# The second half of a modulation summed over k on GpSimd instead of TensorE, in a two-layer mixer kernel

## The reference

```
c_act, cc_act = silu(c), silu(c_ctx)            # two vectors of 2048
mod   = c_act @ w_mod + b_mod                   # w_mod: 2048 x 12288, float32, 100 MB
mod_c = cc_act @ w_mod + b_mod
sh1, sc1, gt1, sh2, sc2, gt2 = split(mod, 6)    # 2048 columns each
csh1, csc1, _, _, _, _ = split(mod_c, 6)
h  = rmsnorm(x, g_norm1) * (1 + sc1) + sh1
hc = rmsnorm(ctx, g_norm1) * (1 + csc1) + csh1
...
x  = x + gt1 * mixer(h, hc)
x  = x + gt2 * conv_ffn(rmsnorm(x, g_norm2) * (1 + sc2) + sh2)
```

## Time and profile before

| | |
|---|---|
| runs | 2424.41, 2425.56, 2426.89 us; median 2425.56 |
| profiled execution | 2423.71 us, of which the span of its instructions is 2421.8 us |
| TensorE busy | 2319.9 us (96%) |
| VectorE busy | 1394.4 us (58%) |
| ScalarE busy | 1043.4 us (43%) |
| GpSimd busy | 77.7 us (3%) |
| DMA | 482.72 MB, 199 GB/s over the span |

### The profile page before, as it was taken

How to read it: one execution, slowest core, us unless ns; L and a number is a source line. 1 busy time by engine, 2 the same in 40 slices (tenths; PEclk the granted TensorE clock), 3 DMA queues, 4 the chain that set the end, 5 groups by cost and what they waited for, 6 DMA issues and landing times.

```text
span 2421.8 us, 30896 instructions
## 1 busy us (share of the span) xinstructions
PE 2319.9 (96%) x10984; PEld 1815.2 (75%) x10984; DVE 1394.4 (58%) x2057; ACT 1043.4 (43%) x1304; POOL 77.7 (3%) x149
## 2 busy tenths in 40 slices
PE   6999999999999899999899999898999999989997
PEld 5677777777777677776588777677888888877886
DVE  5355664444444564353454768756777777775554
ACT  4343435533333334345632444343555555554432
POOL 0000000000001100000000000100000000000000
PEclk9999999999999999999999999999999999999999
DMA  7787777667777878875533322454665665665664
GB/s 243 265 278 253 245 259 242 234 227 222 221 230 253 276 236 284 269 227 170 162 114 105 122 78 87 145 163 160 190 190 174 191 191 172 191 203 179 196 195 131
DMA packets 297374, 482.72 MB, mean 199 GB/s; under 512 B 23074, under 2 KB 114404, under 8 KB 295088
## 3 DMA queue, kind: packets, MB, share of 16 engines
q1 hardware_dynamic: 290824, 464.85, 60.0%
q0 software_dynamic: 6448, 16.48, 2.0%
HBM read 474.56 MB, written 6.69 MB: 199 GB/s over the span
## 4 chain that ended last, share of the span: by engine, by line
PE 85%; DVE 6%; ACT 3%; DMA 3%; issue 2%; SPq 0%; DVEq 0%; POOL 0%; ACTq 0%
PE gemm_ps L1432 71%; PE ps L1459 4%; DMA mraw<-in_w_mod_dram 2%; ACT w_hi L525 2%; DVE w_lo L862 1%; PE ps L1790 1%; PE gemm_ps L1447 1%; DVE tmpT L893 1%; PE ps L1843 1%; PE ps L1927 1%; PE ps L1850 1%; PE ps L1485 1%; DMA w_raw<-in_w_down_dram 1%; PE ps L1795 0%; PE ps L1496 0%
## 5 line engine op out<-in xcount | busy, mean ns | idle before, releaser
L862 DVE TENSOR_TENSOR w_lo<-w_raw,w_hi 128x1024 fp32r<-128x1024 f32 x688 | 831.7, 1223 | 739.0 <-ACT w_hi L525 733.1
L525 ACT ACTIVATE w_hi<-w_raw 128x1024 fp32r<-128x1024 f32 x688 | 713.7, 1054 | 570.0 <-PE gemm_ps L1432 533.8
L1432 PE MATMUL gemm_ps<-w_hi,a_hi 128*128 128x512 f32 (+1 forms) x2304 | 943.7, 410 | 16.0 <-DVE a_lo L900 15.0
L1432 PE MATMUL gemm_ps<-w_lo,a_hi 128*128 128x512 f32 (+1 forms) x2304 | 903.6, 392 | 0.0
L1432 PE MATMUL gemm_ps<-w_hi,a_lo 128*128 128x512 f32 (+1 forms) x2304 | 902.8, 392 | 0.0
L1432 PEld LDWEIGHTS gemm_ps<-w_hi,a_hi 128*128 128x128 f32 x2304 | 437.5, 190 | 173.1 <-issue 56.3
L1432 PEld LDWEIGHTS gemm_ps<-w_hi,a_lo 128*128 128x128 f32 x2304 | 437.6, 190 | 94.1
L1432 PEld LDWEIGHTS gemm_ps<-w_lo,a_hi 128*128 128x128 f32 x2304 | 438.5, 190 | 91.1 <-issue 8.7
L1351 DVE SCALAR_TENSOR_TENSOR acc<-gp,cw,acc 128x256 f32<-128x256 f32 x344 | 151.5, 480 | 13.8 <-DVE acc L1351 1.4
L1432 PE MATMUL gemm_ps<-w_hi,ft_hi 128*128 128x512 f32 x344 | 135.5, 394 | 3.1 <-DVE w_lo L862 3.1
L1432 PE MATMUL gemm_ps<-w_hi,ft_lo 128*128 128x512 f32 x344 | 135.0, 392 | 0.0
(11 more groups left out here) (344 smaller groups left out, 1560.2 us busy)
## 6 DMA issues: line engine op xcount, KB each, us to landing
w_raw<-in_w_in_dram SPq DMA_DIRECT2D x336, 512.0 KB, 4.2
mraw<-in_w_mod_dram SPq DMA_DIRECT2D x192, 512.0 KB, 6.5
w_raw<-in_w_up_dram SPq DMA_DIRECT2D x336, 256.0 KB, 3.0
w_raw<-in_w_down_dram SPq DMA_DIRECT2D x84, 512.0 KB, 4.1
w_raw<-in_w_out_dram SPq DMA_DIRECT2D x64, 512.0 KB, 4.7
w_raw<-in_w_up_dram SPq DMA_DIRECT2D x24, 512.0 KB, 4.0
x_d<-xres POOLq DMA_DIRECT2D x2, 2048.0 KB, 8.3
x_sb<-in_x_dram SPq DMA_DIRECT2D x2, 1024.0 KB, 6.0
```

Of the source, the lines that this page charges most:

```text
L525: act.activation(w_hi[:, slot], raw[:, slot], ACT.Copy).then_inc(hi_done, 1)
L862: dve.tensor_tensor(w_lo[:, slot], raw[:, slot], w_hi[:, slot].bitcast(F32), ALU.subtract).then_inc(lo_done, 1)
L1432: mm = pe.matmul(gemm_ps[:, bank, rt, 0:n], x[:, chunk0 + k, tok], w[:, slot, kk, 0:n], start=(k == 0 and part == 0 and not opened), stop= ...
```

## The change

The first eight column blocks stay as they were, now in 16 groups after unit 7 + 5n of blocks 0 to 10. The other sixteen become eight **sums** of 1024 columns, for the vector c alone. For a sum, SyncE loads one row chunk of 128 by 1024 at a time into a slot of `mraw` (512 KB, 16 chunks). GpSimd multiplies it by `cs[:, j, 0:1]` in place and adds it to `msum`; each instruction waits for the one before by a semaphore. After the sixteenth chunk TensorE folds `msum` over the partitions with two matmuls against ones, into two column groups of `pD`; VectorE copies 64 rows to `mrow`; GpSimd waits for the copy, stores two rows of 2 KB in two DMAs, waits for their landing and begins the next sum. `msum` lies where `relb` was, so the first sum waits until the last logits of the second branch are issued (`h_L`, line 1543).

`sum_places` writes out when: sums 0 and 1 over blocks 12 to 15 (fold 0 after unit 6 of block 13, fold 1 after unit 6 of block 15), sums 2 and 3 in the pair loop (one chunk every two units, the fold after unit 36 of 40, counted from 0; the loop now has two iterations of two), sum 4 in the output projection (fold after its 25th unit), sums 5 and 6 in the context projection (after its 19th and 38th), sum 7 in the x projection (after its 18th). The users of the late columns read one row instead of four partial sums.

The diff, cut; left out are the same edits at the second gate, the smaller waits, and where VectorE and TensorE call the new functions at the places of the two tables.

```diff
+PE_MODS = 8
+SUMS = 8
+SUM_W = 2 * NBLK
+PAIR_SUMS = (2, 3)
 def mod_places():
-    heads = [7 + 16 * n // 3 for n in range(MOD_HEADS)]
-    tail = [8 * (B_OUT + 4) + 8 * n + 4 for n in range(10)]
-    places = heads + [None] * (2 * DC) + [8 * B_OUT + 1 + 16 * n // 3 for n in range(6)] + tail + [8 * (B_X + 4)]
+    places = [7 + 5 * n for n in range(2 * PE_MODS)]
...
+def sum_places():
+    first = {0: (96, 14), 1: (112, 14), 4: (8 * B_OUT + 8, 16), 5: (8 * B_CTX + 2, 17),
+             6: (8 * B_CTX + 21, 17), 7: (8 * B_X + 0, 18)}
+    loads, folds, copies = {}, {}, {}
+    for n, (start, width) in first.items():
+        at = [start + j * width // 16 for j in range(16)]
+        for j in range(16):
+            if j >= 4:
+                fetched = at[j - 4] + 4
+            elif n - 1 in first:
+                fetched = max(first[n - 1][0] + (12 + j) * first[n - 1][1] // 16 + 4, start - 7 + j)
+            else:
+                fetched = start - 6 + j if n == 0 else 8 * B_OUT + j
+            loads.setdefault((fetched // 8, fetched % 8), []).append(16 * n + j)
+        folds[(at[-1] + 1) // 8, (at[-1] + 1) % 8] = n
+        copies[(at[-1] + 1) // 8, (at[-1] + 1) % 8 + 2] = n
+    return loads, folds, copies
...
+    msum = at("msum", [P, 2, NBLK], F32, 189.5)
...
 SyncE
+            def sum_unit(n, j):
+                if isinstance(n, int) and 16 * n + j < SLOTS:
+                    sp.wait_ge(mod_used, BU * (PE_MODS - 1) + 4 + j + 1)
+                else:
+                    sp.wait_ge(sum_used, 16 * n + j + 1 - SLOTS)
+                src = w_mod[:, j, bass.ds(PE_MODS * NBLK + n * SUM_W, SUM_W)]
+                sp.dma_start(mraw[:, j % SLOTS].rearrange("p k c -> p (k c)"), src).then_inc(mod_in[j % SLOTS], 16)
...
+                                at_unit = 2 * PAIR * c2 + PAIR * j + first + i
+                                if at_unit % 2 == 0 and at_unit < 32:
+                                    sum_unit(PAIR_SUMS[0] + n, at_unit // 2)
...
 GpSimd
-            mod_store(0, 15)
+            def sum_row(n, j):
+                pool.wait_ge(mod_in[j % SLOTS], 16 * (2 * PE_MODS + 4 * n + j // SLOTS + 1))
+                row = mraw[:, j % SLOTS]
+                if j == 0:
+                    if n == 0:
+                        pool.wait_ge(mod_used, BU * PE_MODS)
+                        pool.wait_ge(S("h_L"), 2 * HEADS)
+                    else:
+                        pool.wait_ge(sum_fold, n)
+                    pool.tensor_scalar(msum[:], row, cs[:, j, 0:1], None, ALU.mult).then_inc(sum_used, 1)
+                else:
+                    pool.tensor_scalar(row, row, cs[:, j, 0:1], None, ALU.mult).then_inc(sum_scaled, 1)
+                    pool.wait_ge(sum_scaled, 15 * n + j)
+                    pool.wait_ge(sum_used, 16 * n + j)
+                    pool.tensor_tensor(msum[:], row, msum[:], ALU.add).then_inc(sum_used, 1)
+            def sum_store(lo, hi):
+                for n in range(lo, hi):
+                    for j in range(16):
+                        sum_row(n, j)
+                    pool.wait_ge(mod_evac, PE_MODS + n + 1)
+                    for half in range(2):
+                        col = PE_MODS * NBLK + n * SUM_W + half * NBLK
+                        pool.dma_start(mod_d[0, 0:1, col:col + NBLK], mrow[32 * half:32 * half + 1, :]).then_inc(mod_out, 16)
+                    pool.wait_ge(mod_out, 64 * PE_MODS + 32 * (n + 1))
+            sum_store(0, 4)
...
-            mod_store(15, 17)
+            sum_store(4, 5)
             pool.wait_ge(evac_dve, 16)
             pool.dma_start(x1_d, xres[:]).then_inc(S("x1_out"), 16)
-            mod_store(17, MODS)
+            sum_store(5, SUMS)
...
-            pool.dma_start(gtr[0:4], mod_d[:, 0, 2 * D:3 * D]).then_inc(S("gtr_in"), 16)
+            pool.dma_start(gtr[0:1], mod_d[0, 0:1, 2 * D:3 * D]).then_inc(S("gtr_in"), 16)
...
 VectorE
+            def sum_copy(n):
+                dve.wait_ge(sum_fold, n + 1)
+                dve.wait_ge(mod_out, 64 * PE_MODS + 32 * n)
+                dve.tensor_copy(mrow[0:64, :], pD[0:64, :]).then_inc(mod_evac, 1)
...
 TensorE
+            def sum_over_partitions(n):
+                pe.wait_ge(sum_used, 16 * (n + 1))
+                pe.wait_ge(mod_evac, PE_MODS + n)
+                for half in range(2):
+                    mm = pe.matmul(pD[32 * half:32 * half + 32, :], C("strict", P, P, 32), msum[:, half], start=True, stop=True,
+                                   skip_group_check=True)
+                mm.then_inc(sum_fold, 1)
...
-                            after=lambda u: mod_group(11 + j + c, 1 - j) if u == 4 else None)
+                                after=lambda u: sum_over_partitions(PAIR_SUMS[0] + n) if (c2, j, u) == (1, 1, 6) else None)
...
-                            pe.wait_ge(mod_evac, MODS)
+                            pe.wait_ge(mod_evac, PE_MODS + SUMS)
...
```

More of the change, by code:

```diff
@@ L152, in mod_places @@
             copies[(place + 2) // 8, (place + 2) % 8 + 2] = group // 2
-        before = places[group - 1] if group and places[group - 1] is not None else place - 7
         for i in range(4 if group else 0):
-            at = before + 8 + i // 2
-            if place < UP_FIRST:
-                at = min(at, UP_FIRST - 1)
+            at = places[group - 1] + 8 + i // 2
             loads.setdefault((at // 8, at % 8), []).append(4 * group + i)
     return after, loads, copies
-MOD_HEADS = 23
+def sum_places():
[15 more added lines that the diff above has]
+    return loads, folds, copies
 MOD_AFTER, MOD_LOADS, MOD_COPIES = mod_places()
+SUM_LOADS, SUM_FOLDS, SUM_COPIES = sum_places()
 class Count:
@@ L355, in of @@
                         mod_unit(unit_of // BU, unit_of % BU)
+                    for row in SUM_LOADS.get((block, i), ()):
+                        sum_unit(row // 16, row % 16)
                 return of
@@ L980, in mod_copy, with modulation @@
                 dve.tensor_copy(mrow[:, :], pD).then_inc(mod_evac, 1)
+            def sum_copy(n):
+                dve.wait_ge(sum_fold, n + 1)
+                dve.wait_ge(mod_out, 64 * PE_MODS + 32 * n)
+                dve.tensor_copy(mrow[0:64, :], pD[0:64, :]).then_inc(mod_evac, 1)
+            def modulation(block, i):
+                if (block, i) in MOD_COPIES:
+                    mod_copy(MOD_COPIES[block, i])
+                if (block, i) in SUM_COPIES:
+                    sum_copy(SUM_COPIES[block, i])
             dve.memset(gbias[:, :], EPS).then_inc(S("eps_set"), 1)
@@ L1023, in _ @@
                         splits(2 * B, i, i + 1)
-                        if (B, i) in MOD_COPIES:
-                            mod_copy(MOD_COPIES[B, i])
+                        modulation(B, i)
                         if seg:
@@ L1466, in modulation @@
                     mod_group(group // 2, group % 2)
+                if (block, u) in SUM_FOLDS:
+                    sum_over_partitions(SUM_FOLDS[block, u])
             def turn(use, src, scaled, first, g):
```

130 lines of the change are left out of this document (65 added, 65 removed).

## The result

The changed kernel takes 2568.89 us (median of 4 runs, 2564.39 to 2571.3) against 2424.98 us for the kernel before in the same session: ratio 1.0595, interval 1.0575 to 1.0615. It is 6% slower. The forecast was 2480 us, slower, with a range from 2355 to 2515: the sign was right, the size was not.

The account below looks back on a forecast made before the run. TensorE, busy 96% of the span, was taken as the bound: 2423.7 - 77.7 removed + 7.7 folds + 125 lateness at folds = 2479 us, plus 1.9 above the profiled execution, 2480; range 2355 to 2515.

Parts of the forecast that it names:

- The ceiling: Whole kernel if GpSimd hides all its work: 2423.7 - 77.7 + 7.7 = 2354 us profiled, 2356 us as run.
- The removed groups and the folds: On TensorE: 32 modulation groups go, 64.6 us plus 13.1 idle; eight folds add 7.7 us (up to 15.8).
- Which folds are late: TensorE waits for GpSimd at folds 0, 1, 4, 5, 6 and 7, not 2 and 3: 125 us together.
- the prediction's own windows: TensorE's time from GpSimd's possible start to each fold: 63.4, 57.5, 118 (folds 2 and 3), 50, 56.4, 53.3, 93 us.
- the price of the scaling: GpSimd's scaling of a 128x1024 row chunk costs 1.054 us, taken from ScalarE's one-operand copy.
- The addition's 2.29 us: GpSimd's addition of a row chunk, high end, operands fetched in turn: 0.162 + 2 x 1.062 us; low end 1.224.
- strict turns: GpSimd and VectorE's splits exclude each other at SBUF for whole instructions, adding 1.23 us per split to GpSimd's time; chance 0.52.
- No turns, low price: GpSimd works beside VectorE undisturbed: 2371 us, or 2356 with the low price of a row chunk; chance 0.32.
- Its deciding point: The no-turns rival decides once a row chunk with its splits takes less than about 4.2 us instead of 4.8.
- The third rival: VectorE becomes the bound, 2.9 us a unit against TensorE's 2.75: above 2515 us; chance 0.06.
- fourth rival: DMA near its limit in the windows adds up to 15 us; sign: TensorE idle before units, ended by weight DMAs.

Follow-up runs that it names:

- 8-column kernel: Changed kernel with GpSimd's scaling and addition cut to 8 of 1024 columns, all DMAs, waits, folds and stores kept: 2367.4 us, ratio 0.9755.
- half the columns: Changed kernel with GpSimd's scaling and addition on 512 of 1024 columns, the first chunk of a sum whole: 2398.3 us.
- the kernel with the wide windows: Changed kernel with 14 column blocks on TensorE and five GpSimd sums, each over 30 units or in the pair loop: 2452.1 us, ratio 1.0112.

## Why the prediction was right in sign and short in size

**The ceiling** (2356): 2367.4 measured. The 13.1 us of idle time did not all go; 8.9 us of waits for mraw before modulation groups are left where the forecast left 2.8, for the groups that stay are read every 5 units (with the old spacing 3.5 us are left, in the kernel with the sums on VectorE). That is 6 of the 11 us; the rest was not followed. The removed groups and the folds were sized right: the modulation's matmuls are 256 records and 32.4 us where some 32 were forecast, and the folds took 1.05 us where TensorE had not idled before (0.96 forecast) and 1.92 after a wait, still inside the 15.8 us allowed.

**Which folds are late.** Right, all eight: six late, the pair loop's two not (0.9 us between them). The lateness was read by subtracting the fold's start in the 8-column kernel from its start in the changed kernel, and taking the increase from fold to fold. The middle column puts the measured duration of each sum (from its first scaling to the fold) into the prediction's own windows, with the measured restart (8.3, 8.2 and 5.2 us for sums 1, 6 and 7). TensorE's waits right before the folds, which the prediction put at 8 to 31 us each, were only 1.0 to 12.0, since most of the lateness gathers between the units.

```
fold   GpSimd's sum, us        late, us
       forecast   measured     forecast   window, measured sum   measured
0        79.3       90.0         15.9            26.6               25.2
1        75.2       85.8         25.2            36.6               38.2
2, 3      -          -            0               0                  0.9
4        74.6       88.4         24.6            38.4               38.9
5        77.0       85.7         20.6            29.3               36.8
6        77.0       85.0         31.2            39.9               40.1
7        93.5      107.6          8.0            19.8               17.6
sum                             125             190.6              197.8
```

So the windows were right to 8 us in all (that of fold 5 alone was 7.5 us too long), and the miss is in GpSimd's sum: some 8 to 14 us each. Lateness is a difference of sum and window, so sums that are 12% too short gave a lateness that is 37% too small.

**The step that failed: the price of the scaling.** It was put at 1.054 us from ScalarE's copy. It lasts 2.84 us undisturbed (the nine that no split overlaps are within 0.02 us of that), in the changed kernel:

```profile
L507 POOL TENSOR_SCALAR mraw<-mraw,cs x120: 2836/2850/4893, 363.4 to 1262.8; 128x1024 f32<-128x1024 f32 x120
...
L510 POOL TENSOR_TENSOR msum<-mraw,msum x120: 2337/2394/3326, 366.3 to 1265.7; 128x1024 f32<-128x1024 f32 x120
```

(shortest, median and longest ns.) The addition's 2.29 us was right: 2337 at the shortest. The Trainium skill's figure that stood beside it (GPSIMD Engine Reference, Performance versus the Vector engine), 4497 ns for 2048 columns, agrees too: half of it is an estimated 2.25 us. The same page of the Trainium skill, section Engine selection, calls a one-input operation on GpSimd roughly line-rate; the trace disagrees: the one-input scaling is GpSimd's dearer instruction, 2.84 us against 2.34. No bound of the prediction reached 2.84 us, although the same reasoning that took the high end for the addition (nothing shows GpSimd the faster engine) was at hand for the scaling.

**The second term, wrong the other way: strict turns.** Fifteen chunks of 5.25 us and a first scaling of 2.85 are 81.6 us; the five late sums other than the last took 85.0 to 90.0, so meetings with VectorE added 3 to 8 us a sum, not 23. Turns exist: the median scaling is 2.85 us but some last 4.89, and splits last up to 3.44 us. In the pair loop (GpSimd, then VectorE):

```profile
643.63 2.40 POOL L510 TENSOR_TENSOR msum<-mraw,msum 128x1024 f32<-128x1024 f32 x1
646.00 4.87 POOL L507 TENSOR_SCALAR mraw<-mraw,cs 128x1024 f32<-128x1024 f32 x1
...
644.19 4.05 DVE L923 TENSOR_TENSOR w_lo<-w_raw,w_hi 128x1024 fp32r<-128x1024 f32 x2 [1.30 <-ACT w_hi L586]
```

The first of the two splits starts while GpSimd adds and ends only at 647.1; the scaling that starts before that end takes 2 us longer than alone. But the split of 1.23 us at 1241.35, shown above, lies wholly inside a scaling of 2.85 us, and neither is longer than when alone. The rule of the Trainium skill (SBUF — State Buffer, Who interferes with whom), exclusion for the whole length, thus agrees with the trace in part: it would give longer instructions at each meeting, and the spans show them at some.

Which meetings cost shows when the starts in the changed kernel's trace are counted ("longer" is by over 0.1 us than 2.84, 2.34 and 1.22 us). It is the instruction that starts second. Of GpSimd's scalings, all 43 that start while a split runs are longer, and 6 of the other 77; of its additions 23 of 25, and 5 of the other 95. Of the splits, 35 of the 40 that start while GpSimd adds are longer (2.63 us in the mean), but only 32 of the 132 that start while it scales (1.32), and one of the other 516 (1.22). So a split was held up by the two-operand addition and mostly not by the one-operand scaling, and the forecast charged both in full. GpSimd's spans in a profile are rough, and why the scaling lets most splits pass is left open. The kernel with one-operand splits shows that a second operand isn't needed for a meeting to cost (694 ns in the median, up to 2887).

There was a reason besides for so few turns: SyncE, held at an mraw slot, delivers one unit per chunk, so VectorE has one split per 5.25 us in those windows. The slowdown thins out its own interference. In the pair loop, where the units keep their pace, splits and scalings lengthen each other most (1.75 and 4.28 us in the mean in the kernel with the pair loop's sums alone).

**Together**: lateness came to 201.5 us by the medians, 125 forecast. The price gives 28 us a sum (81.6 against 53.6) and the turns take back some 18, net 10 us for each of five sums, 52 us in all. The last sum is 14 us longer, which one wait accounts for: the fifth of its chunks came 14.6 us late, because SyncE issued it only after eight units of weights that stand ahead of it in its order (1160.4 to 1192.5 us), though its slot was free:

```profile
1197.42 3.36 POOL L507 TENSOR_SCALAR mraw<-mraw,cs 128x1024 f32<-128x1024 f32 x1 [14.60 <-DMA mraw<-in_w_mod_dram]
```

The windows give 7 us more, and 4 us lie between the last fold's lateness and the medians. The 11 us of the ceiling come on top.

That the forecast missed by only 89 us is partly luck, for its two errors pull against each other. With the measured price and its own strict turns the same sum gives 43.9 + 53.2 + 52.6 + 48.6 + 59.2 + 36 us of lateness and twice 25 in the pair loop, 344 us, so about 2699 us, 130 too many.

**The rivals.** "No turns, low price" lost on its price, though its premise is nearer to the trace than the forecast's: with 81.6 us a sum and no turns at all, the windows and the measured restarts give 18.2 + 32.4 + 31.6 + 25.2 + 36.5 + 0 = 144 us, so 2500 us, inside the forecast's range: a time there would not have told turns from a dear scaling. Its deciding point, 4.2 us a chunk, is not contradicted: with half the columns (3.6 us a chunk) the time is 2398, under that of before. The third rival named VectorE as the bound with TensorE idle between units; the idle time is there (55.0 us for splits), but behind it stand the weights that SyncE holds back, the sign that the prediction gave to its fourth rival, and wasn't priced. In the pair loop the units keep their pace and the splits are longest, and there nothing is lost. DMA bandwidth was not the bound: the changed kernel moved 231 GB/s in the last window, below the 272 of the 8-column kernel at the same work (its 1005 to 1065 us):

```profile
1200.00:1260.00 60.00, 53.88 (x292) 43.04 (x292) 30.60 (x32) 24.20 (x27) 59.08 (x22) 0.97 0.69 231
```
```profile
1005.00:1065.00 60.00, 59.42 (x326) 48.48 (x325) 28.00 (x38) 25.99 (x30) 12.60 (x24) 0.97 0.79 272
```

## What to carry to other kernels

An engine that has never computed in a trace has no price there: bound every one of its instructions by the dearest reading, not only the one that looks hard (here even that, 2.29 us, would have fallen short of 2.84), and look for the engine that does the whole step in one instruction first (here VectorE, 1.28 against 5.25 us). Where work is handed to a slower engine, compare its whole sum with the window of the engine that waits: past the window each us counted in full here, inside it only what the engine takes from its neighbours (4.9 us of waits for splits with the pair loop's sums alone, 29.5 in the kernel with the wide windows). And a queue that loads for both, in a fixed order, spreads the slow engine's lateness over the fast one's inputs, so the wait is seen far from its cause.

## What the runs showed of the hardware

- GpSimd on 128x1024 float32: product with a per-partition factor 2.84 us, with a constant 2.76, addition of two tiles 2.34, product of two operands with one repeated 1.88 at the shortest. The shortest are 1.55 and 1.26 us for scaling and addition of 512 columns, 0.30 and 0.19 for 8: from these sizes an estimated 2.5 and 2.1 ns a column, so the scaling's surplus grows with the columns and only 0.1 us of it is fixed. (On 8 columns the scaling's mean is 0.76 us, because half of them start while a split runs.)
- VectorE's product and addition in one instruction costs 1.28 us for 128x1024, only 0.05 more than a subtraction.
- GpSimd beside VectorE lengthened VectorE's splits from 1222 to 1323 ns in the mean, with the addition alone as much as with both instructions, and to 1520 ns beside two-operand products. The lengthened ones are nearly all splits that start while a two-operand instruction of GpSimd runs (35 of 40 during an addition, 90 of 95 during a two-operand product, 32 of 132 during a one-operand scaling), and GpSimd's instructions are lengthened when they start while a split runs (66 of 68, against 11 of 172).
- The same fold took 1.05 us after work and 1.92 us after an idle stretch (granted clock 1.00 and 0.50 in these stretches). In the window from 451 to 555 us, where TensorE was busy 78 of 104 us, the granted clock was 0.81 in the mean, against 0.97 in the 8-column kernel (102 of 104 us busy).
